# A one-core layer step: pipelined opening, token pick after the down product, and a last projection that starts tile by tile

## The reference

```python
xn = RMSNorm(x, g_mix); proj = xn @ w_in      # z | xBC | dt | gate_y | x_lru | gate_m | gate_r
dt = softplus(dt_raw + dt_bias)               # step sizes of the SSD branch, cumulated per chunk
x = x + mixed @ w_o                           # mixed: the SSD and the RG-LRU branch, gated
x = x + hier_moe(RMSNorm(x, g_ffn))           # 32 experts (2048 -> 512 -> 2048), two for each token
ple_gate = sigmoid(RMSNorm(x, g_ple) @ w_ple_gate)
x = x + ple_gate * (p @ w_ple)
return RMSNorm(x, g_final), and the new states
```

## Time and profile before

| | us |
|---|---|
| median of 3 runs | 3111.93 (3105.14 to 3112.49) |
| the profiled execution | 3108.33 |
| its span, first to last instruction | 3106.5 |
| first projection of group 0 starts | 49.8 |
| expert loop, from the first wait for an up weight to the last down product | 1881 to 2855 |
| last projection, PE busy | 2900.8 to 3089.8 |
| last instruction of DVE ends | 3102.0 |

### The profile page before, as it was taken

The page is one execution under the profiler, slowest core; times in us unless marked ns, Lnnn a source line. Parts: engine busy times, 40 slices in busy tenths (PEclk is TensorE's granted clock), DMA queues, the critical chain, the costliest instruction groups (busy, mean ns, idle before and its releaser), DMA issues.

```text
span 3106.5 us, 33721 instructions
## 1 busy us (share of the span) xinstructions
PE 2868.2 (92%) x14019; PEld 1858.4 (60%) x14019; DVE 538.2 (17%) x1103; ACT 368.4 (12%) x633; POOL 51.8 (2%) x79
## 2 busy tenths in 40 slices
PE   6999999999999999999999989889988988996797
PEld 3656565555555555555557875555555555554686
DVE  3333433323322000000000011001000100011311
ACT  2111121212222000000001020000000000000101
POOL 1000000000000000000001000000000000000000
PEclk8989899999999999999999999999999999998899
DMA  7344343332332333232336328999999999998322
GB/s 156 106 141 124 109 136 105 118 95 88 107 96 86 103 108 108 91 98 93 96 108 234 122 82 361 423 422 414 421 423 422 422 417 426 426 426 329 109 81 95
DMA packets 228561, 646.76 MB, mean 208 GB/s; under 512 B 7805, under 2 KB 196741, under 8 KB 209221
## 3 DMA queue, kind: packets, MB, share of 16 engines
q1 hardware_dynamic: 209904, 600.07, 50.8%
q0 software_dynamic: 6560, 27.55, 3.3%
q10 hardware_dynamic: 12058, 18.61, 1.6%
HBM read 616.17 MB, written 30.04 MB: 208 GB/s over the span
## 4 chain that ended last, share of the span: by engine, by line
PE 82%; DMA 14%; DVE 2%; ACT 1%; issue 1%; POOL 0%; DVEq 0%; POOLq 0%; ACTq 0%; SPq 0%
PE bank L1322 21%; PE bank L1213 13%; PE bank L1422 11%; DMA arena<-in_w_exp_up_dram 11%; PE bank L1292 11%; PE bank L1401 6%; PE bank L1361 5%; PE bank L1456 5%; PE bank L1440 4%; DMA arena<-in_x_sample_dram 1%; PE bank L1272 1%; PE bank L1458 1%; DMA arena<-in_state_ssm_dram 1%; PE bank L1276 1%; DMA out_dram<-arena 0%
## 5 line engine op out<-in xcount | busy, mean ns | idle before, releaser
L1322 PE MATMUL bank<-arena 128*128 128x384 f32 x2048 | 660.6, 486 | 0.0
L1322 PEld LDWEIGHTS bank<-arena 128*128 128x128 f32 x2048 | 389.1, 190 | 271.4
L1422 PE MATMUL bank<-arena 128*64 128x256 f32 x4096 | 469.8, 390 | 66.4 <-DMA arena<-in_w_exp_up_dram 38.7
L1422 PEld LDWEIGHTS bank<-arena 128*64 128x64 f32 x4096 | 304.9, 141 | 241.5 <-DMA arena<-in_w_exp_up_dram 46.0
L1213 PE MATMUL bank<-arena 128*128 128x384 f32 x1280 | 414.5, 486 | 0.0
L1213 PEld LDWEIGHTS bank<-arena 128*128 128x128 f32 x1280 | 242.7, 190 | 169.3 <-issue 2.1
L1292 PE MATMUL bank<-arena 128*128 128x384 f32 x1024 | 330.9, 486 | 0.0
L1292 PEld LDWEIGHTS bank<-arena 128*128 128x128 f32 x1024 | 194.6, 190 | 135.9 <-issue 0.5
L1440 PE MATMUL bank<-arena 128*64 128x512 f32 x1024 | 231.6, 605 | 29.5 <-DVE arena L1114 23.2
L1401 PE MATMUL bank<-arena 128*128 128x128 f32 x1632 | 189.1, 278 | 4.0 <-ACT arena L715 4.0
L1401 PEld LDWEIGHTS bank<-arena 128*128 128x128 f32 x1632 | 185.9, 194 | 10.2 <-issue 6.2
(11 more groups left out here) (313 smaller groups left out, 1314.1 us busy)
## 6 DMA issues: line engine op xcount, KB each, us to landing
arena<-in_w_exp_gate_dram SPq DMA_DIRECT2D x32, 4096.0 KB, 19.0
arena<-in_w_exp_up_dram SPq DMA_DIRECT2D x32, 4096.0 KB, 21.3
arena<-in_w_exp_down_dram SPq DMA_DIRECT2D x32, 4096.0 KB, 17.6
arena<-in_w_in_dram SPq DMA_DIRECT2D x48, 2048.0 KB, 8.3
arena<-in_w_out_m_dram SPq DMA_DIRECT2D x8, 2048.0 KB, 8.1
arena<-in_w_out_r_dram SPq DMA_DIRECT2D x8, 2048.0 KB, 8.1
arena<-in_w_o_dram SPq DMA_DIRECT2D x8, 2048.0 KB, 8.2
expert_rows<-arena ACTq DMA_DIRECT2D x64, 256.0 KB, 13.2
```

The costliest lines, as they stand in the source:

```text
L1322: last = mm(banks[2 * s + cc][:, 0:T], slab[s % 2][:, k, cc * 128:(cc + 1) * 128], rhs[:, k, :], start=(k == 0), stop=(k == KC - 1))
L1422: last = mm(banks[2 * x + i][h * SLOTS:(h + 1) * SLOTS, 0:FF // 2], xe[:, k, x * SLOTS:(x + 1) * SLOTS], w[:, k, h * (FF // 2):(h + 1) * ( ...
```

## The change

It has four parts.

- Opening. `d_skip` is loaded as one row of 32 numbers to 128 partitions, and DVE later copies every second number into place. `w_dt` is issued behind the slabs X0 and X1. ACT issues the parameter loads ahead of the squares. The three tiles have three staging buffers and a separate square output; DVE does statistics and scale of tiles 0 and 1 before it evicts tile 0, and ACT scales tile 2. The history and parameter transposes, the dt product, the dt sum and `dt_columns` are moved in between the projections of group 0: behind the 1st, 2nd, 3rd and 5th. The step-size arithmetic goes behind the second convolution on DVE and behind the third copy on ACT. SP waits for `dt_tr` at the same place of its list as before.
- Experts. `pick_tokens` and `xe_columns` of the next pair go behind the down product of x = 1.
- Last projection. The second addition of each tile is made in two halves; PE transposes the unscaled `x_res` half by half, ACT multiplies by the gain as it evicts (16 blocks of 128x128 for each tile), the row factor goes into the sigmoid's scale, and the units are ordered by slab pair, tile, half. Tiles 1 and 2 are transposed after units 0 and 1. Four slab buffers replace two; the first two slabs and `w_ple` are loaded during the last down product.
- Output. Squares are summed for each unit, `gfin` is multiplied in advance, and at a tile's last unit the factor is applied to columns 0 to 1279 by DVE and to the rest by ACT; SP and ACT store their parts.

```diff
-            sp.dma_start(w_dt, w_in[0, :, OFF_DT:OFF_DT + HEADS].rearrange("(k p) c -> p k c", p=128)).then_inc(dt_loaded, 16)
...
                 load_slab(0, w_in, g * 512 + OFF_X, proj_done, 10 * g + 1)
                 load_slab(1, w_in, g * 512 + OFF_X + SLAB, proj_done, 10 * g + 2)
+                if isinstance(g, int):
+                    sp.dma_start(w_dt, w_in[0, :, OFF_DT:OFF_DT + HEADS].rearrange("(k p) c -> p k c", p=128)).then_inc(dt_loaded, 16)
                 sp.wait_ge(cum_stored, 16)
                 sp.wait_ge(dt_tr, 1)
...
+            load_ple(0, 0)
             sp.dma_start(w_ple_sb, a["w_ple"][0].rearrange("(k p) c -> p k c", p=128)).then_inc(ple_in, 16)
+            load_ple(0, 1)
+            for h in range(2):
+                sp.wait_ge(comb_done, n_pass * COMB + 1 + 3 * (h + 1))
+                sp.sem_inc(wait_stop, 1)
+                load_ple(1, h)
...
-            for half in range(2):
-                pool.dma_start(dskip[half * 64:(half + 1) * 64, :],
-                               a["d_skip"][0].rearrange("(c h) -> h c", h=2)[half].partition_broadcast(64),
-                               allow_slow_non_contiguous=True).then_inc(setup_in, 16)
+            pool.dma_start(skip_rows, a["d_skip"][0].partition_broadcast(128)).then_inc(setup_in, 16)
...
+            for t in range(2):
+                norm_stats(t)
+                norm_scale(t, x_in[:, t, :], staging(t))
+            norm_evict(0, P_GMIX, xnT, 0)
+            norm_stats(2)
+            norm_evict(1, P_GMIX, xnT, 1)
+            norm_evict(2, P_GMIX, xnT, 2)
...
+                opening = {0: history_and_params, 1: dt_partial, 2: dt_sum, 4: dt_columns} if isinstance(g, int) else {}
...
                         last.then_inc(proj_done, 1)
+                        if m + c in opening:
+                            opening[m + c]()
...
-                        if x == 1:
-                            pick_tokens(p * PAIRS + q + 1)
...
+                    pick_tokens(p * PAIRS + q + 1)
...
+            def tile_transposes(t):
+                for half in range(2):
+                    pe.wait_ge(comb_done, n_pass * COMB + 3 * t + 3 + half)
+                    pe.sem_inc(wait_stop, 1)
+                    for b in (2 * half, 2 * half + 1):
+                        if t:
+                            pe.wait_ge(xp_evac, 4 * (t - 1) + b + 1)
+                        for q in range(4):
+                            k = 4 * b + q
+                            last = tr(banks[b][:, q * 128:(q + 1) * 128], x_res[:, t, k * 128:(k + 1) * 128], ident)
+                        last.then_inc(xp_tr, 1)
+
+            tile_transposes(0)
+            for u, (i, t, h) in enumerate(units):
...
+                if u < 2:
+                    tile_transposes(u + 1)
...
+            for u, (i, t, h) in enumerate(units):
+                act.wait_ge(ple_mm, u + 1)
+                A(gsig[u % 2], banks[4 + u % 4][:, 0:SLAB], ACT.Sigmoid, scale=q_rstd[:, t:t + 1]).then_inc(ple_sig, 1)
+                if (i, h) == (3, 1):
+                    A(sm[:, 60 + t:61 + t], ones[:, 0:1], ACT.Sqrt)
...
+                    TS(yfin[t][:, 0:YCUT], yfin[t][:, 0:YCUT], f_rstd[:, t:t + 1], None, ALU.mult).then_inc(f_ok, 1)
```

More of the change, by code:

```diff
@@ L36 @@
 PAIRS = NE // 2
+COMB = 3 * NT
 PLE = 256
@@ L570, in _ @@
             assert n == PARAM_DMAS, n
-            act.wait_ge(consts_ready, CONSTS)
[L573 to L592, removed]
+            for t in range(NT):
+                act.wait_ge(x_loaded[t], 16)
+                if t:
+                    act.wait_ge(n_sq, t)
+                square_tile(t, x_in[:, t, :], squares)
+            act.wait_ge(n_rc, NT)
+            A(staging(2), x_in[:, 2, :], ACT.Identity, scale=sm[:, rstd_c + 2:rstd_c + 3]).then_inc(n_scaled, 1)
+            act.wait_ge(consts_ready, CONSTS)
             def to_padded(n, nconv, m):
@@ L615, in _ @@
                     to_padded(10 * g + m, 6 * g + m, m)
+                    if first and m == 0:
+                        history()
                     if m:
                         silu(m - 1)
+                    if first and m == 2:
+                        time_steps()
                 silu(5)
@@ L746, in _ @@
             for t in range(NT):
[L747 to L760, removed]
@@ L762, in _ @@
-            for t in range(NT):
-                act.wait_ge(f_out[t], 16)
+                for b in range(4):
+                    act.wait_ge(xp_tr, 4 * t + b + 1)
+                    for q in range(4):
+                        k = 4 * b + q
+                        last = A(xn2T[:, k, t * 128:(t + 1) * 128], banks[b][:, q * 128:(q + 1) * 128], ACT.Identity,
+                                 scale=pcol[:, P_GPLE + k:P_GPLE + k + 1])
+                    last.then_inc(xp_evac, 1)
+                if t:
+                    act.wait_ge(q_sq, t)
@@ L1108, in expert_pair @@
                            ALU.mult).then_inc(h_mul, 1)
-                        if x == 1:
-                            for b in range(4):
-                                xe_columns(p * PAIRS + q + 1, b)
                         dve.wait_ge(h_tr, E + 1)
@@ L1114, in expert_pair @@
                         V.tensor_copy(hid[x], v3(banks[2 * x + 1][:, FF // 2:FF], FC)).then_inc(gu_done, 1)
+                    for b in range(4):
+                        xe_columns(p * PAIRS + q + 1, b)
                 dve.sem_inc(wait_stop, 1)
@@ L1142, in _ @@
[L1142 to L1148 removed]
+            dve.wait_ge(q_sq, NT)
@@ L1183, in _ @@
-            pe.wait_ge(n_evac, 12 + 4)
-            tr(banks[3][:, 0:128], sm[:, 0:128], ident).then_inc(hist_T, 1)
-            pe.wait_ge(dt_loaded, 16)
-            for k in range(KC // 4):
-                for j in range(4):
-                    last = mm(banks[4][32 * j:32 * j + HEADS, 0:T], w_dt[:, 4 * k + j, :], xnT[:, 4 * k + j, :],
-                              start=(k == 0), stop=(k == KC // 4 - 1))
-            last.then_inc(dt_part, 1)
-            pe.wait_ge(params_in, 16 * PARAM_DMAS)
@@ new lines, in dt_partial, with dt_sum @@
+            def dt_partial():
+                pe.wait_ge(dt_loaded, 16)
+                for k in range(KC // 4):
+                    for j in range(4):
+                        last = mm(banks[4][32 * j:32 * j + HEADS, 0:T], w_dt[:, 4 * k + j, :], xnT[:, 4 * k + j, :],
+                                  start=(k == 0), stop=(k == KC // 4 - 1))
+                last.then_inc(dt_part, 1)
+            def dt_sum():
+                pe.wait_ge(dt_sel, 2)
+                mm(banks[5][0:HEADS, 0:T], sel, dt4, start=True, stop=True).then_inc(dt_done, 1)
@@ new lines, in _ @@
+            tile_transposes(0)
+            for u, (i, t, h) in enumerate(units):
+                bank, w = banks[4 + u % 4], ple_slab[i % 2][h]
+                pe.wait_ge(pslab[2 * (i % 2) + h], 16 * (i // 2) + 16)
+                pe.wait_ge(xp_evac, 4 * t + 4)
+                if u >= 4:
+                    pe.wait_ge(ple_done, u - 3)
+                for k in range(KC):
+                    mm(bank[:, 0:SLAB], xn2T[:, k, t * 128:(t + 1) * 128], w[:, k, :], start=(k == 0), stop=(k == KC - 1))
+                if u == 0:
+                    pe.wait_ge(ple_in, 16)
+                for k in range(2):
+                    last = mm(bank[:, SLAB:2 * SLAB], pT[:, k, t * 128:(t + 1) * 128], w_ple_sb[:, k, i * 512 + h * SLAB:i * 512 + (h + 1) * SLAB],
+                              start=(k == 0), stop=(k == 1))
+                last.then_inc(ple_mm, 1)
+                if u < 2:
+                    tile_transposes(u + 1)
```

323 lines of the change are left out of this document (189 added, 134 removed).

## The result

The changed kernel takes 3063.29 us, the median of four runs (3060.54 to 3065.51). The kernel before, run beside it, takes 3109.37 us (3105.14 to 3112.49). The ratio is 0.9844, with a 95% interval from 0.9828 to 0.9860: 46.1 us less. The forecast was 3070, with a range of 3052 to 3085.

A forecast was written before the change was run, and what follows sets the result against it. PE products held 82% of the chain of waits, DMA 14%; transfers bound the expert loop. Terms 2.5 + 6 + 6 + 18.5 + 7.9 = 40.9 us off 3108.3 gave 3067.4, put at 3070; range 3052 to 3085.

The forecast's parts named there:

- Rival (c): Opening: x_sample stays late because small pieces as such, not d_skip, hold the engines; 3085 us, chance 0.08.
- Rival (a): Opening: slab Z0 comes in time, so the opening keeps its 12 us; 3060 us, chance 0.12.
- rival (b): Expert loop gives nothing and the row store behaves as in the loop; 3080 us, chance 0.10.
- (d): Expert loop turns from transfers to PE, slower than before; 3126 us at 3.5 us late, chance 0.02.
- (e): Last projection: unit 2 or 4 waits for ACT's evictions, 5 to 8 us; 3077 us, chance 0.10.
- The opening: Until projection 7: earlier projections, less a new 8.8 us PE wait for slab Z0; gain 2.5 us, -3 to +12.
- hidden by nothing, no gain: Opening: the moved PE work, 9.0 us, is still PE work between projections, so no gain and no loss.
- The loop: Expert loop: down load goes out 11 us earlier and the silence ahead of it goes; gain 6 us, 0 to 8.
- so the queue stays full: Expert loop: next gate load, 1.7 us later, still precedes the end of the transfer ahead, about 0.5 us to spare.
- The end of the loop: Last down product starts 9.2 us earlier, less row-store slowdown beside SP's loads; gain 6 us, between 2 and 9.2.
- The last projection: Gather to unit 0 shortens by 23.5 us, 5.0 back for transposes between units; gain 18.5 us, 14 to 20.
- The tail: Behind the last product: 4.4 us of work instead of 12.25; gain 7.9 us, from 6 to 9.

The follow-up runs named there:

- the two `d_skip` kernels: Changed kernel with the old 4-byte load of d_skip, 3079.21 us; kernel before with only the new one-row load of d_skip, 3096.43 us.

## Why the prediction was right, and where it wasn't

**Size and direction.** The time is 6.7 us below the forecast and inside the range. Some of that nearness is luck: the terms of the opening and of the last projection were 10.7 us too low, those of the loop and its end 4.4 us too high, and the reason given for the loop's term was wrong. Rival (c), x_sample held by small pieces as such, those of `w_dt` too, falls with the two `d_skip` kernels. Rival (a), Z0 in time, falls with the trace: PE waited 9.5 us. It is what the kernel becomes when Z0 is queued first. Of the 10 us that rival (b) takes off, 4.4 came true: less in the loop and less at its end. Rivals (d) and (e) did not occur: the loop did not grow, and unit 0 ran 16.2 us behind the gather, as forecast.

**The opening.** The new wait was right in cause and size: 9.5 us for 8.8. Its neighbours were mis-sized. `dt_tr` came at 87.1, not 89.7: the moved work took 7.2 us instead of 9.1, mostly because the dt product takes 2.72 us between projections where it took 4.4, and the first projection came 0.7 us sooner. Z0 landed 20.0 us behind it, not 19.2. The clock allowance of 1.5 us ahead of projection 7 was used up: the first five projections took 53.35 us, not 51.8, with a granted clock of 0.82 from 40.1 to 46 us. The one behind the wait was nearly right too: projections 7 and 8 took 22.55 instead of 20.64 us, 1.9. At projection 9 the gain is 3.9. The other 5.5 up to the expert stage are 4.4 in the tail of group 0 and 1.1 later, which was not followed up. The term failed there: I took the tail of group 0 to move with its start, and the two traces grant it a clock of 0.90 and 0.77. The higher clock came with the wait in four traces of four, so the step "hidden by nothing, no gain" holds for the work but not for the clock behind it.

**The loop.** 4.0 us for 6, of which, as above, not even the 4.0 is shown to be the pick's. The step "so the queue stays full" is wrong, in the pair shown and in the count. I placed the next gate load against the transfer ahead of it as that transfer ran before, begun at about 2051. Once the down load goes out 11 us earlier, its transfer also ends 11 us earlier, and the gate load is late by nearly the whole pick. I should have moved both ends of the comparison. The sign that no such stretch of the loop would have a DMA share below 0.5 was therefore wrong as well.

**The end of the loop.** 3.6 us for 6. The product started 8.6 us earlier against its weights (9.2 forecast) and the row store lost 3.3 us (3.2 taken, between 1 and 7.5). The last down product itself took 8.80 us instead of 7.11, at a lower clock: 1.7 us that no step held. Before, PE came to it out of 11 us of pick; after, out of a wait. That alone doesn't decide it, though. The unchanged repeat came to it out of the same wait and took 7.11 us; there it was unit 0 that ran longer:

```profile
2825.22 7.11 PE bank L1516 x32
...
2857.61 8.75 PE bank L1542 x32
```

In that execution the stretch takes 16.3 us, 5.3 less than before. So the step that was mis-sized is mainly the clock of one product in one execution; the row store's price was right.

The prediction had estimated about 8 us for this term from the turns between queues, packet by packet, that the Trainium skill (DMA: Bandwidth & Descriptors, Queues, rings and completion order) states; the loop's row gave 2. The trace has neither: the store took 6.36 us beside the slab loads and 3.08 alone, so it lost 3.3 us where the estimate had it lose 1.2. The page's rule fits in direction, since the store was served beside three loads already queued; the size was the prediction's own estimate, and too small.

**The last projection.** From the gather to unit 0 the steps held to 0.1 us. The 32 transposes between units cost 3.5 us, not 5.0 (1.75 for each tile, without the waits that were in the old ones), and unit 0 took 7.15 instead of 9.44. Unit 0's clock is not the change's own: it took 8.75 us in the unchanged repeat, 8.81 with Z0 first and 10.15 with the pick at its old place. So of the 3.8 us more than forecast, 1.5 are a price that I took too high and 2.3 are the clock of this run.

**The tail.** 8.1 us for 7.9, and 4.3 us behind the last product for 4.4. The steps are those of the trace.

**The sum.** New `d_skip` alone gives 12.3 us, the pick alone 14.1, and the last projection with its tail 30.5 by the two traces: 56.9, where the change gave 46.1. Two things account for most of the difference. The pipelined opening with its wait starts group 1 at 189.02, 3.5 us later than new `d_skip` alone (185.49); with Z0 first it starts it 3.8 us earlier (181.71). So of the opening's gain nothing comes from the pipelining as it stands. And loop and loop's end give 7.6 us in the changed kernel where the pick alone had 13.9 (978.6 and 16.0 in the table), 2.0 of it at the end, where no `w_ple` and slab loads ran beside the last stores (3.3 us) but its last down product took 1.2 us longer, and the rest in the loop's own variation.

## What to carry to other kernels

Before a step is moved later on one engine, list what is queued behind each wait for its result: here a weight slab stood behind such a wait on SP's queue, and one line that issues it first is worth 6 to 8 us. When work is moved past a product in a loop that transfers bound, compare the next load with the transfer ahead of it at its new time too; the silence moved to the next buffer and did not go. And look in a slow opening for a transfer with pieces of one element: 8 KB of them cost this kernel 12 us.

## What the runs showed that I had not expected

- The 4-byte pieces of `d_skip`, 8 KB in two transfers from POOL's queue, hold a 1 MB load on SP's queue for 15 to 18 us (30.1 to 31.0 us to landing in three kernels with them, 12.9 to 14.8 in six without), while 2048 pieces of 128 bytes behind the same load on its own queue do nothing of the kind.
- With a wait of 9.5 us in group 0, the tail of that group, which starts 45 us behind it, spent 6.8 us at 1.2 GHz instead of 17.1 or more, and took 36.4 to 36.6 us in four traces with the wait and 39.8 to 41.4 in five without. The stall is paid for twice at its place (9.5 and 1.9 us), and some of it seems to be given back. What decides it stays open.
- A store of 256 KB takes 3.07 to 3.10 us alone, 6.3 to 6.4 us beside the slab loads at the end, and 10.6 to 21.1 us beside the expert loads. Only the first two differ by one thing.
- Over the whole span the lower clock was granted for 201 us before and for 150 us after. Some of that lies in waits of PE, where it costs nothing. How much of the 47.5 us is clock, these runs don't separate.
